# Second layer's output projection: first 512 input rows for both column blocks ahead of the turning of the differential heads

## What is computed

```python
def odd_mixer(h_lat, h_ctx, w_in, ..., subln_g, w_out, lam_init, cos, sin, need_ctx):
    ...
    def merge(yc, yd):
        yd = rms_norm(yd, subln_g) * (1.0 - lam_init)
        return jnp.concatenate([merge_heads(yc), merge_heads(yd)], -1) @ w_out
    ...
    y_lat = merge(window_gqa(cq_l, ck_l, cv_l, ck_c, cv_c, sink),
                  diff_attention_latent(dq_l, dk_l, dv_l, dk_c, dv_c, lam))
```

## Time and profile before

| what | us |
|---|---|
| median of 3 runs | 2944.88 |
| lowest and highest | 2943.93, 2949.64 |
| profiled execution, first to last instruction (span) | 2938.9 |
| PE busy in it | 2766.3 (94%) |
| DVE busy in it | 1832.5 (62%) |
| ACT busy in it | 1517.6 (52%) |
| mean granted TensorE clock | 0.966 |

### The profile page before, as it was taken

The page is one execution under the profiler, slowest core; times in us unless marked ns, Lnnn a source line. Parts: engine busy times, 40 slices in busy tenths (PEclk is TensorE's granted clock), DMA queues, the critical chain, the costliest instruction groups (busy, mean ns, idle before and its releaser), DMA issues.

```text
span 2938.9 us, 34671 instructions
## 1 busy us (share of the span) xinstructions
PE 2766.3 (94%) x13289; PEld 2282.2 (78%) x13289; DVE 1832.5 (62%) x2326; ACT 1517.6 (52%) x2155; POOL 155.1 (5%) x204
## 2 busy tenths in 40 slices
PE   6998899999998869999999899999699999998899
PEld 5777678878886558888888788787578888787787
DVE  5676665666677545545788855569655555546555
ACT  5563455545554224444677645574354455564453
POOL 2111000000030000000000000002000000100100
PEclk8999999999999869999999999999899999999999
DMA  7673256656662015555799855551055655551444
GB/s 269 229 249 99 69 193 211 219 196 222 223 188 65 1 58 179 158 179 175 270 320 334 305 165 172 173 186 43 24 182 165 209 186 168 205 180 43 136 157 143
DMA packets 266291, 510.45 MB, mean 174 GB/s; under 512 B 9268, under 2 KB 40204, under 8 KB 266139
## 3 DMA queue, kind: packets, MB, share of 16 engines
q1 hardware_dynamic: 262336, 498.11, 50.8%
q0 software_dynamic: 3808, 10.35, 1.2%
HBM read 507.33 MB, written 1.05 MB: 173 GB/s over the span
## 4 chain that ended last, share of the span: by engine, by line
PE 84%; DVE 8%; ACT 3%; DMA 2%; issue 1%; POOL 1%; ACTq 0%; DVEq 0%; SPq 0%; POOLq 0%
PE bank L416 23%; PE bank L417 23%; PE bank L420 22%; PE bank L1324 2%; PE bank L1337 2%; DVE wlo L324 2%; DVE h_hid L2571 1%; PE bank L1350 1%; PE bank L387 1%; ACT whi L320 1%; PE bank L389 1%; PE bank L388 1%; PE bank L2117 1%; PE bank L510 1%; DMA raw<-in_moe_w 1%
## 5 line engine op out<-in xcount | busy, mean ns | idle before, releaser
L324 DVE TENSOR_TENSOR wlo<-raw,whi 128x1024 fp32r<-128x1024 f32 (+1 forms) x1012 | 1195.6, 1199 | 785.6 <-ACT whi L320 781.1
L320 ACT ACTIVATE whi<-raw 128x1024 fp32r<-128x1024 f32 (+1 forms) x1012 | 1037.5, 1040 | 815.2 <-PE bank L420 771.5
L416 PE MATMUL bank<-whi,xhi 128*128 128x512 f32 (+2 forms) x2328 | 888.9, 382 | 22.2 <-DVE wlo L324 8.9
L420 PE MATMUL bank<-whi,xlo 128*128 128x512 f32 (+2 forms) x2328 | 879.2, 378 | 0.0
L417 PE MATMUL bank<-wlo,xhi 128*128 128x512 f32 (+2 forms) x2328 | 879.2, 378 | 0.0
L416 PEld LDWEIGHTS bank<-whi,xhi 128*128 128x128 f32 x2328 | 442.5, 190 | 107.4 <-issue 21.1
L420 PEld LDWEIGHTS bank<-whi,xlo 128*128 128x128 f32 x2328 | 441.8, 190 | 78.1
L417 PEld LDWEIGHTS bank<-wlo,xhi 128*128 128x128 f32 x2328 | 442.0, 190 | 74.7
L416 PE MATMUL bank<-whi,f_hhi 128*128 128x512 f32 x496 | 197.6, 398 | 3.1 <-ACT f_gates L971 3.1
L417 PE MATMUL bank<-wlo,f_hhi 128*128 128x512 f32 x496 | 196.6, 396 | 0.0
L420 PE MATMUL bank<-whi,f_hlo 128*128 128x512 f32 x496 | 196.4, 396 | 0.0
(11 more groups left out here) (532 smaller groups left out, 2892.4 us busy)
## 6 DMA issues: line engine op xcount, KB each, us to landing
raw<-in_ffn_w SPq DMA_DIRECT2D x180, 1024.0 KB, 5.1
raw<-in_moe_w SPq DMA_DIRECT2D x96, 1024.0 KB, 5.6
raw<-in_ada_w SPq DMA_DIRECT2D x48, 1024.0 KB, 6.2
raw<-in_moe_w SPq DMA_DIRECT2D x48, 768.0 KB, 4.7
raw<-in_ev_w_in SPq DMA_DIRECT2D x24, 1024.0 KB, 5.7
raw<-in_ffn_w SPq DMA_DIRECT2D x36, 512.0 KB, 3.6
raw<-in_hyb_w_in SPq DMA_DIRECT2D x18, 1024.0 KB, 5.0
raw<-in_attn_w_qkv SPq DMA_DIRECT2D x18, 1024.0 KB, 5.1
```

The costliest lines, as they stand in the source:

```text
L320: nc.scalar.activation(whole, part, ACT.Copy).then_inc(sem("w_hi"), 1)
L324: nc.vector.tensor_tensor(wlo[s][:, 0:rows, 0:n], part, whole.bitcast(F32), ALU.subtract)\
L416: nc.tensor.matmul(bank[:, 0:n], xk_h, whi[s][:, wk, 0:n], start=first, stop=False)
L420: ins = nc.tensor.matmul(bank[:, 0:n], xk_l, whi[s][:, wk, 0:n], start=False, stop=last)
```

## The change

On PE, the two units of rows 0 to 511 (of the first and of the second column block) are written ahead of the turning of the differential heads, and the two units of rows 512 to 1023 behind it. The sums of the blocks stay open in banks 0, 1 and 2, 3 in between. SP loads the four units in this new order. ACT splits the third and fourth unit ahead of taking out the turned heads, and takes both blocks' sums at the end. DVE splits a unit ahead of each of its two cuts. No instruction is added or left out.

```diff
+    OUT_ORDER = [(k0, c) for k0 in (0, 4) for c in range(2)]
+    def odd_out_pe(e, s, k0):
+        for c, banks in enumerate((G, U)):
+            s.unit(xhi, xlo, k0, 4, N, banks, k0 == 0, k0 == 4)
+        e.outs.n += k0 // 4 * 2
+    def odd_out_act(e, s):
+        for c, banks in enumerate((G, U)):
+            def take():
+                for t in range(NT):
+                    ins = nc.scalar.activation(y[:, t, c * N:c * N + N], banks[t][:, :], ACT.Copy)
+                ins.then_inc(sem("out_done"), 1)
+            s.step(take)
+        e.outs.n += 2
...
-                project_load(ld, a["od_w_out"][0], D, D)
+                for k0, c in OUT_ORDER:
+                    ld.unit(tiles(a["od_w_out"][0], k0, 4, c * N, N), 4, N)
...
+                expert_shapes(s, 4)
+                s.step()
+                s.step()
                 e.after("sublng")
                 heads_out_act(e, "att_d", 4, sublng[:, 0:1])
-                expert_shapes(s, 4)
-                project_act(e, s, D, D, lambda t, c, n: y[:, t, c:c + n])
+                odd_out_act(e, s)
...
-                cut_x(e, "cat_o", range(2, 4), lambda b: f"att_d:oT{b}")
                 expert_shapes(s, 4)
-                project_dve(e, s, D, D)
+                for b in range(2, 4):
+                    s.step()
+                    cut_x(e, "cat_o", (b,), lambda b: f"att_d:oT{b}")
+                for _ in range(2):
+                    s.step()
+                e.outs.n += 2
...
+                follow(e, s, "cat_o")
+                odd_out_pe(e, s, 0)
                 heads_out_pe(e, "att_d")
-                follow(e, s, "cat_o")
-                project_pe(e, s, [(xhi, xlo, KD)], D, "out_o")
+                odd_out_pe(e, s, 4)
```

## The result

| | before | after |
|---|---|---|
| median, us (runs) | 2943.31 (6) | 2930.53 (6) |
| lowest and highest | 2938.71, 2949.64 | 2922.82, 2935.19 |
| ratio after to before | | 0.9949, 95% interval 0.9934 to 0.9964 |
| span of the profiled execution | 2938.9 | 2928.7 |

What follows compares the result with a forecast made beforehand. With PE busy 94% of the span, only its idle or lower-clock time could be won: 10.9 us of matmuls off the path, plus 2.0 from the clock, minus 3.5 of pauses, gives 9.4; forecast 2935.5 us, range 2932.5 to 2940.

Steps and rivals of the forecast that it cites:

- The gap: PE's 11.85 us idle between attention and transposes: 48 matmuls were to run there, 10.9 us hidden whole.
- ACT's roundings: Four roundings of the third and fourth unit, 1.06 each, done before the transposes end; priced at nothing, cover 0.9 us.
- the first pause behind the transposes: PE idle before the third unit's first half, waiting for DVE's splits and first cut; a cost of 2.6 us.
- the second pause: PE waiting after the third unit's first 12 matmuls for DVE's second cut; a cost of 0.9 us.
- The first rival: PE's clock falls in the short new pauses around the transposes; gain 7.2 to 8.9, time 2936.0 to 2937.7; chance 0.35.
- so the whole rest moves up by 9.4: Everything behind the gates' matmul hangs on this chain and was to start 9.4 us earlier, span 2929.5.
- The prediction's own sign of being wrong: Wrong if transposes start over 12 us after attention, attention to gates exceeds 33, or the stretch behind the gates grew longer.
- 6.0 us below the median's: Distance of the profiled span from the runs' median (2944.88), kept to turn span 2929.5 into time 2935.5.
- rival 2: DVE's chain up to the second cut is longer than its parts; gain 4 to 7, time 2938 to 2941; chance 0.08.
- rival 3: Early units right behind the attention run at half clock, 20.5 us; slower, 2953 with all slow; chance 0.03.
- rival 4: Early units wait and PE's order holds the transposes back, or the gain is hidden; time 2944 to 2945; chance 0.05.
- rival 5: Gain of more than 10 us, only if DVE's chain got shorter; time 2932 to 2934.8; chance 0.04.

Runs made afterwards that it cites:

- pause_filled: Changed kernel with ten added matmuls of 128x512 between the transposes and the third unit; median 2930.46 us, ratio to before 0.9967.
- after_again: The changed kernel, unchanged, timed again in more rounds; median 2933.50 us, ratio to before 0.9957.
- after_delayed: Changed kernel with 38 added matmuls on PE between the projection and the gates' matmul; median 2944.03 us, ratio to before 1.0007.
- after_shift: Changed kernel with 8 added matmuls (1.8 us) between the projection and the gates; median 2937.23 us, ratio to before 0.9980.
- after_shift_b: Changed kernel with 8 added matmuls between the projection and the gates, run once more; median 2936.46 us, ratio to before 0.9974.
- after_shift15: Changed kernel with 15 added matmuls (3.4 us) between the projection and the gates; median 2935.97 us, ratio to before 0.9964.
- after_router_warm: Changed kernel with 24 added matmuls behind the gates and 24 behind the router; median 2928.90 us, ratio to before 0.9953.
- split_halves: Changed kernel with DVE's order finer: half split, first cut, half split, second cut, last two splits; median 2932.86 us, ratio to before 0.9975.
- split_in_root: Changed kernel with DVE's first two weight splits moved into its wait for POOL's root, the last two behind both cuts; 2932.31 us, ratio 0.9956.
- all_warm: Changed kernel with finer DVE split order, 8 added matmuls behind the transposes and 48 in the router's stretch; 2928.54 us, ratio 0.9951.
- before_again: The kernel before, unchanged, as a second sample; median 2943.23 us, ratio to before 0.9996.

## Why the prediction was wrong where it was

**The gap, the prices and the order of events were right.** 48 matmuls ran straight behind the attention at steps of 0.227, hidden whole; PE idle 0.94 before the transposes; transposes 1.09; DVE's chain unchanged with company; ACT's roundings no cost (the last ended at 1042.03, the transposes at 1042.96); the first pause behind the transposes 2.46 us. Only the second pause was mis-sized: 0.35 us with the clock kept up, priced at 0.9.

**The first rival happened.** The clock fell in the pauses. Priced at a gain of 7.2 to 8.9, it came out at 8.6 in after's profile against before's, 8.3 against the mean of three. pause_filled measures the fall itself: 1.0 us (priced at 1.1 to 1.8). It was given 0.35 and the forecast 0.45; in all nine profiles that have the new order and nothing added in the pause (after, after_again, after_delayed, after_shift, after_shift_b, after_shift15, after_router_warm, split_halves, split_in_root) the clock fell there, for 3.4 us in seven and for 6.8 in two (after_shift_b, split_in_root); in the two with the pause filled (pause_filled, all_warm) it did not. What the Trainium skill's page "TensorE: Matmul & The Clock Gate" says in the passage named with that rival, that short idle moments make the clock swing, agrees with these eleven profiles.

**The step that failed** is this one: "Nothing there goes by a clock of its own, so the whole rest moves up by 9.4." The rest did not simply move up. The router's stretch costs 37 or 41 to 42 us by whether the clock rises around the start of the router's matmuls (at the latest 0.84 us behind it, in before_again) or stays low through them (3.8 to 4.0 or 6.8 us for the same 32). Which of the two it is went, in all sixteen profiles, by how far behind the clock's fall after the gates the norm's transposes start: short at 3.0 to 3.8 us and at 5.9 to 6.2, long at 4.3 to 5.4. The new order alone lay in the short groups five times of five, the old one time of three. The router's stretch has a mean of 40.4 in three profiles of the old order and 37.1 in two of the new: 3.4 us. Middle stretch and router's stretch together are 8.3 + 3.4 = 11.7 us, and the three measured differences are 12.8, 10.3 and 11.5. With two to three profiles a side and intervals of some 4 us to either side, this sum fits and is not proven; that the change moved this stretch, and not chance alone, rests on the kernels with added work. The direction was chance as far as the profile before could tell; that the place could answer with 4 us could be suspected from its trace, where the clock stood at 0.5 for 34 us (1062.7 to 1096.8). The prediction's own sign of being wrong, a stretch behind the gates that has become longer, looked the other way.

**A smaller miss**: I took the profiled execution's time to lie 6.0 us below the median's because of what lies around the span, and carried that over. In every run with both numbers it is 1.8 (2930.53 with a span of 2928.7). The profiled execution of before was simply a quicker one, by about its 2.6 us below the median of six, and my starting point of 2944.88 was 1.6 above that median. Without this the same gain would have been 2933.9, and the measured time still 3.4 below; the range, lowered by the same 1.6, would begin at 2930.9, and the time would still lie under it.

**The rivals that did not happen**: DVE's chain was not longer than its parts (rival 2), though split_in_root shows that a split beside POOL's root makes it so; the early units were never slow (rival 3); the order did what it says (rival 4). A gain over 10 us (rival 5, 0.04) was tied to a shorter DVE chain, which was not its cause.

**What stays open**: how often the router's stretch is short in either kernel was read from a few profiles, not counted over the timed runs; why the clock fell at another time behind the gates in the one order than in the other, and whether the borders at about 4 and 5.7 us hold under further delays, was not tried; and the time to the attention's end differs by up to 4.5 us between profiles of one program and by 12 between all the kernels, which I did not take apart.

## What to carry to other kernels

Fill a gap of the matrix engine to its end or expect little: half of the work in the gap was worth 1.3 us and the whole 8.3, because the idle rest still let the clock fall and a pause behind the transposes kept it low. Before trusting that the rest of a program just moves up, look at the stretches behind the change that run at the low clock: each is a place that may cost more or less when it is reached at another time, and adding work of two or three different lengths ahead of it tests that. And don't subtract the end points of two single profiles; subtract the stretches, and profile the kernel before more than once.

## What the hardware showed that I had not expected

- Between medians a delay of 1.8 us cost 3 to 7 us, one of 3.4 no more than that, and 1.8 us of added work made the other kernel no slower. In the profiles of the new order the router's stretch went from 37 to 41 us and back to 37 with these delays, by the granted clock.
- The norm's sixteen transposes started at the same time within 0.05 us in two executions, and the clock rose at their end in the one (it had fallen 3.8 us ahead of them) and stayed at 0.50 in the other (5.4 us).
- 32 matmuls of 128x8 kept PE "busy" for 6.83 to 6.84 us at a granted clock of 0.50 (1.2 GHz) in eight of sixteen profiles, and took 3.80 to 4.04 in the other eight.
- POOL's TENSOR_SCALAR on 128x8 took 1.16 instead of 0.20 us and its TENSOR_TENSOR 2.48 instead of 1.64, with DVE's two-input subtraction beside them, while DVE's own time did not change (2.36 for two).
